# Lighter VectorE steps in the opening, and state-space matrices loaded as whole rows and turned by TensorE, in a two-layer encoder kernel

## The chip, the cores and the metric

The kernel runs on one core of one Trainium2 chip. The metric is the device time of one execution in microseconds (us). The kernel before was timed in three runs: median 1413.44 us, from 1413.34 to 1413.91 us. The profile is of one further execution.

## What is computed

A trunk of two layers over 256 tokens of width 1024, all in float32:

```python
for layer in range(2):
    proj = rms_norm(x) @ w_in[layer]            # q, k, v, u and two gates
    q, k = rotary(q), rotary(k)
    a = diff_attention(q, k, v, lam)            # 4 heads, two softmaxes, lam scales the second
    s = s5_bidirectional(u, ...)                # 32 groups of 16 channels, 64 complex states each
    x = x + (gates[0] * (a @ w_branch[0]) + gates[1] * (glu(s) @ w_branch[1])) @ w_out
    x = x + (swiglu(rms_norm(x)) if layer == 0 else top2_of_8_experts(rms_norm(x)))
out = rms_norm(x)
```

The state-space mixer is where the change lies. For each direction d, group g and state p it has a decay `a_bar = exp(lam * dt)`, an input matrix `b_bar = ((a_bar - 1) / lam) * b_mat` (state by channel) and an output matrix `c_mat` (channel by state):

```python
bu = einsum('gph,bsgh->bsgp', b_bar, u)
states = scan(a_bar, bu)                        # one direction runs backwards
y = u * d_skip + real(einsum('ghp,bsgp->bsgh', c_mat, states))
```

`lam` of the attention is `exp(sum(lp[0]*lp[1])) - exp(sum(lp[2]*lp[3])) + lam_init`, a number for each layer.

## The kernel before, in words

Weights come as tiles of 128x2048 through three raw buffers. ScalarE (ACT) rounds each to a part `hi` (`split`, L1215), VectorE (DVE) makes the rest `lo` (L1632), and TensorE (PE) multiplies with three matmuls for each product (`three`, L659; `proj`, L678). The DMA of a tile waits until the tile three places before it has its `lo` (L543). Tiles 0 and 1 of the opening are the columns of u, 2 and 3 those of v, 4 and 5 of q, 6 and 7 of k, 8 and later of the gates. Each engine has its own program, written out in order; semaphores join them.

The scan is done in chunks of four tokens, so powers 0 to 4 of `a_bar` times the input matrices are needed, and powers 0 to 3 times the output matrices. In layer 0 the powers of the input matrices are made on DVE (`input_power`, L1739), those of the output matrices on POOL (`c_chain`, L2234). In layer 1 POOL makes both.

The opening, layer 0, engine by engine, as far as the change and the prediction touch it:

- POOL issues eight DMAs with the input matrices in runs of 16 numbers (`load_matrices(0)`, L2211), four with the output matrices, each matrix twice (`load_states`, L2217), and four with the skip weights (`load_dskip`, L2224). Then it waits for `par`, makes phasors (`phasors`, L452), the powers of the output matrices, more phasors and the first rotation table (`phase_products`, L2242), and signals `wtab_half` (L2255).
- ACT copies the input matrices into the PSUM banks PY (L1373), and the turned output matrices out of the turn banks TR, two copies of 64 partitions for each bank (`state_numbers`, L1301).
- PE multiplies tiles 0 and 1, turns the seven rows of parameters ("par", L843), multiplies tile 2, turns the output matrices (`states_numbers_t`, L793, 16 transposes of 128x128 in four banks), multiplies tile 3, turns u, multiplies tiles 4 to 7, turns the rotated q, and runs `inner` (L754), which waits for `b_part`, `kdiag_ready` and `c_ready`. Then it turns the rotated k and, in eight banks, the powers (L870, the B turns).
- DVE makes the parameters, splits tiles 2 and 3, makes the attention's lambda sums (L1998, L1999), copies the turned parameters to SBUF (L2002), and goes into `mixer(0)` (L1827): the four factors (`next_factor`), powers 0 and 1, tile 4, power 2, tiles 5 and 6, `rotary` of q, tile 7, powers 3 and 4, the diagonal of the skip weights (`inner_diagonal`, L1758: two operations of 16 partitions), `rotary` of k, tiles 8 and 9.
- ACT in the B turns stops after the fourth one for `scan_tables(0)` (L1321), which waits for `wtab_half`, and copies the rest afterwards.

`rotary` (L1682) reads a projection from its PSUM bank PJ, writes one product of 512 columns and one crossed product of 2x256 to SBUF, gives PJ free for the next projection (`pj_free`, L1698), and adds the two. The output matrices of layer 1 are turned near the end of layer 0's mixer, between the tiles 22 and 23 (L935).

Of the kernel before, what the change touches and what calls it, by code (L numbers as in the profile page):

```python
# [18 lines left out]
P = 128  # L19
# [3 lines left out]
HEADS, HD = 4, 64  # L23
# [19 lines left out]
C_ID, C_TRI, C_ONE, C_IOTA, C_SEL, C_COS, C_SIN = 0, 128, 256, 384, 513, 641, 769  # L43
C_ROW, C_SLOT, C_END = 897, 899, 900
# [79 lines left out]
def build(nc, x, norm_mix, w_in, attn_lambda, attn_subln, ssm_lam_re, ssm_lam_im, ssm_log_dt, ssm_b_re, ssm_b_im,  # L124
# [6 lines left out]
    with ctx:  # L131
# [66 lines left out]
        braw, bbar = powers(area(0, 1024)), powers(area(TMP + 2048, 1024))  # L198
        bt = [powers(area(1024 + 1024 * i, 1024)) for i in range(2)]
        pt = [powers(area(c0, 1024)) for c0 in (14592, TMP)]  # L200
        craw = [area(c0, 1024).rearrange("p (i a s) -> p i a s", i=8, a=2) for c0 in (8192, TMP + 1024)]
# [206 lines left out]
        dve_mark, power_mark = small[:, 20:21], small[:, 21:22]  # L408
        dve_rows, sel_early, inv_ready = sem("dve_rows"), sem("sel_early"), sem("inv_ready")
        B_LOADS, C_LOADS = 16 * 8, 16 * 4  # L410
# [244 lines left out]
        def _(pe):  # L655
# [137 lines left out]
            def states_numbers_t(l):  # L793

                pe.wait_ge(c_in, C_LOADS * (l + 1))
                for g in range(4):
                    transposes((l, "ct", g), [craw[g // 2][:, 4 * (g % 2) + i, :, :].rearrange("p a s -> p (a s)") for i in range(4)])
# [34 lines left out]
            def mixer(l):  # L832
# [375 lines left out]
        def _(act):  # L1208
# [132 lines left out]
            def mixer(l):  # L1341
# [284 lines left out]
        def _(dve):  # L1626
# [55 lines left out]
            def rotary(l, name, dst):  # L1682
                i = place_of(l, name)

                cos_t, sin_t = (cst[:, c:c + 128].rearrange("p (t c) -> p t c", t=2) for c in (C_COS, C_SIN))
                for th in range(TH):
# [5 lines left out]
                    own.step(stt(a_flat[:, 0:512].rearrange("p (h c) -> p h c", c=HD), src.rearrange("p (h c) -> p h c", c=HD),  # L1692
# [721 lines left out]
```

## Time and profile before

| | us |
|---|---|
| median of 3 runs | 1413.44 |
| lowest and highest | 1413.34, 1413.91 |
| the profiled execution | 1413.13 |
| its span, first to last instruction | 1411.3 |
| PE busy | 1371.2 (97%) |
| DVE busy | 1107.8 (78%) |
| ACT busy | 895.1 (63%) |
| POOL busy | 358.3 (25%) |
| mean granted TensorE clock | 0.996 of full |

Busy time of PE counts matmuls in a pipeline from issue to modelled end, so 97% is not the peak. The parts of an engine's time that matter are those which the chain of work that ended last goes through. PEld is PE's weight load. In a line of the trace `out<-in` names the tensors (most of the SBUF areas of the mixer lie in `raw`, `gates` and `areg`), and `[... <-X]` is idle time before the instruction and what ended it.

### The profile page before, as it was taken

Reading aid. Unit: us, or ns where it says so; the run is one execution under the profiler, and the core shown is the slowest. Engines: PE = TensorE matmul, PEld = TensorE weight load, DVE = VectorE, ACT = ScalarE, POOL = GpSimd, SP = SyncE. Lnnn points to the kernel's source line nnn. Section 1 sums busy time; section 2 is a strip of 40 time slices with the busy share of each in tenths; the row PEclk is TensorE's granted clock in tenths of the full one; section 3 lists DMA queues with packets and bytes.
Section 4 is the critical chain, followed back from the end, with each engine's and each line's share of the span. In section 5 each row is a group of like instructions: output and inputs, shape, how many; then the busy total and the mean of one; then the engine's idle time right before and its main releaser. Section 6 shows DMA issues by size and latency. Waiting matters only on the chain.

```text
span 1411.3 us, 23368 instructions
## 1 busy us (share of the span) xinstructions
PE 1371.2 (97%) x8481; PEld 1122.8 (80%) x8481; DVE 1107.8 (78%) x1021; ACT 895.1 (63%) x903; POOL 358.3 (25%) x459
## 2 busy tenths in 40 slices
PE   6889999999999999999999999999999999999996
PEld 4778778788888787788888888888888888888885
DVE  6987677655556587678888888889888888898886
ACT  5445555444445455556777777777777777777775
POOL 4988718996000187000000000000000000000100
PEclk9999999999999999999999999999999999999998
DMA  9433365655545242697999999999999999999991
GB/s 243 159 95 130 113 187 164 207 181 193 193 168 189 57 172 91 235 330 283 365 373 371 389 377 378 386 359 386 384 365 389 382 373 386 360 383 352 384 355 30
DMA packets 194804, 385.16 MB, mean 273 GB/s; under 512 B 17969, under 2 KB 57265, under 8 KB 194610
## 3 DMA queue, kind: packets, MB, share of 16 engines
q1 hardware_dynamic: 188256, 367.51, 72.9%
q0 software_dynamic: 4336, 14.17, 4.0%
q10 hardware_dynamic: 2146, 2.59, 0.6%
q8 instruction: 43, 0.70, 0.2%
q14 instruction: 23, 0.19, 0.0%
HBM read 375.83 MB, written 7.34 MB: 272 GB/s over the span
## 4 chain that ended last, share of the span: by engine, by line
PE 88%; DVE 5%; ACT 3%; issue 2%; DMA 1%; ACTq 0%; POOL 0%; SPq 0%; DVEq 0%; POOLq 0%
PE bank L657 84%; DVE lo L1632 2%; ACT hi L1215 2%; PE bank L1109 1%; PE bank L675 1%; DMA raw<-in_w_in_dram 1%; PE bank L776 1%; DVE raw L1749 0%; PE bank L1092 0%; DVE bank L1751 0%; PE bank L814 0%; DMA areg<-in_norm_mix_dram 0%; PE bank L983 0%; ACT at_hi L1539 0%; DVE areg L1695 0%
## 5 line engine op out<-in xcount | busy, mean ns | idle before, releaser
L1632 DVE TENSOR_TENSOR lo<-raw,hi 128x2048 fp32r<-128x2048 f32 x347 | 803.1, 2326 | 161.3 <-ACT hi L1215 159.1
L1215 ACT ACTIVATE hi<-raw 128x2048 fp32r<-128x2048 f32 x347 | 663.8, 1916 | 183.9 <-PE bank L657 178.1
L657 PE MATMUL bank<-hi,at_hi 128*128 128x512 f32 x1288 | 513.5, 399 | 13.3 <-DVE lo L1632 8.0
L657 PE MATMUL bank<-hi,at_lo 128*128 128x512 f32 x1288 | 503.4, 391 | 0.0
L657 PE MATMUL bank<-lo,at_hi 128*128 128x512 f32 x1288 | 502.6, 390 | 0.0
L657 PEld LDWEIGHTS bank<-hi,at_hi 128*128 128x128 f32 x1288 | 242.5, 188 | 67.9 <-DVE lo L1632 13.3
L657 PEld LDWEIGHTS bank<-hi,at_lo 128*128 128x128 f32 x1288 | 242.1, 188 | 52.1
L657 PEld LDWEIGHTS bank<-lo,at_hi 128*128 128x128 f32 x1288 | 242.7, 188 | 47.3
L657 PE MATMUL bank<-hi,ht_hi 128*128 128x512 f32 x432 | 168.8, 391 | 0.9 <-DVE ht_lo L2116 0.9
L657 PE MATMUL bank<-hi,ht_lo 128*128 128x512 f32 x432 | 168.1, 389 | 0.0
L657 PE MATMUL bank<-lo,ht_hi 128*128 128x512 f32 x432 | 168.1, 389 | 0.0
L2343 POOL TENSOR_TENSOR small<-cst 128x1 f32<-128x1 f32 x14 | 5.9, 422 | 590.7 <-DVE slot_row L2153 298.6
L657 PEld LDWEIGHTS bank<-hi,ht_hi 128*128 128x128 f32 x432 | 81.1, 188 | 19.2 <-DVE lo L1632 1.5
L657 PEld LDWEIGHTS bank<-hi,ht_lo 128*128 128x128 f32 x432 | 81.1, 188 | 17.0
L657 PEld LDWEIGHTS bank<-lo,ht_hi 128*128 128x128 f32 x432 | 81.1, 188 | 16.6
L1548 ACT ACTIVATE ht_hi<-bank 128x512 fp32r<-128x512 f32 (+1 forms) x48 | 26.9, 560 | 55.6 <-PE bank L1109 55.6
L2273 POOL TENSOR_TENSOR raw<-raw 128x256 f32<-128x256 f32 x64 | 46.8, 762 | 21.6 <-ACT raw L1332 7.6
L1544 ACT ACTIVATE vreg<-bank 128x512 f32<-128x512 f32 (+1 forms) x48 | 27.1, 565 | 25.1 <-PE bank L657 25.1
L657 PEld LDWEIGHTS bank<-raw 64*64 64x64 f32 x1152 | 36.1, 134 | 7.6 <-issue 4.4
L657 PE MATMUL bank<-raw 64*64 64x64 f32 x1152 | 40.5, 221 | 0.0
L2266 POOL MEMSET raw<- 128x4 f32 x4 | 0.3, 104 | 151.9 <-DVE raw L1726 151.9
L1227 ACT ACTIVATE at_hi<-bank 128x512 fp32r<-128x512 f32 x32 | 17.7, 596 | 33.3 <-PE bank L675 33.3
(304 smaller groups left out, 1150.8 us busy)
## 6 DMA issues: line engine op xcount, KB each, us to landing
raw<-in_moe_w_dram SPq DMA_DIRECT2D x528, 512.0 KB, 6.8
raw<-in_ffn_w_dram SPq DMA_DIRECT2D x66, 512.0 KB, 4.2
raw<-in_w_in_dram SPq DMA_DIRECT2D x64, 512.0 KB, 4.5
raw<-in_w_branch_dram SPq DMA_DIRECT2D x16, 512.0 KB, 4.4
raw<-in_w_out_dram SPq DMA_DIRECT2D x16, 512.0 KB, 4.7
raw<-in_w_glu_dram SPq DMA_DIRECT2D x4, 512.0 KB, 4.1
moe_sum<-xres POOLq DMA_DIRECT2D x3, 512.0 KB, 5.4
xres<-in_x_dram SPq DMA_DIRECT2D x2, 512.0 KB, 6.5
```

Source lines behind the costliest of these rows:

```text
L657: return pe.matmul(o, a, b, start=start, stop=stop)
L675: last = pe.transpose(bank[:, i * rows:(i + 1) * rows], src, ident[0:rows, 0:rows])
L776: m = pe.matmul(bank[r0:r0 + GC, c0:c0 + 64], bbar[rows, r, q, d, :], cblk[rows, r, q, 4 * d:4 * d + 4, :].rearrange("p i h -> p (i h)"), ...
L1109: m = pe.transpose(TR[0][:, f * P:(f + 1) * P], v_flat[:, f * P:(f + 1) * P], ident)
L1215: act.activation(hi[:, slot, :], src, ACT.Copy).then_inc(hi_ready, 1)
L1227: act.activation(at_hi[:, k0:k0 + kn, c0:c0 + P], bank[:, 0:kn * P].rearrange("p (k c) -> p k c", k=kn), ACT.Copy, scale=scale).then_inc(a ...
L1544: act.activation(v_flat[:, 0:h_width(c)], PJ[0][:, 0:h_width(c)], ACT.Silu).then_inc(g_ready, 1)
L1548: act.activation(ht_rows_hi[:, 0:h_width(c) // P, :], TR[0][:, 0:h_width(c)].rearrange("p (f s) -> p f s", s=P), ACT.Copy).then_inc(ht_hi_ ...
L1632: tt(lo[:, slot, :], src, hi[:, slot, :].bitcast(f32), SUB).then_inc(lo_ready, 1)
L2266: pool.memset(edge[:, :, :, 0:1], 0.0)
L2273: last = tt(dst, src[:, :, :, d, :], w[:, r:r + 1, :, d, :].broadcast_to([P, 2, 2, 64]), MUL)
L2343: tt(small[:, 82 + i:83 + i], ident[:, 0:1], ident[:, 0:1], MUL).then_inc(pool_passed, 1)
```

## The change

- **Input matrices, layer 0.** Two DMAs, one for each of the real and imaginary parts, bring whole rows of 4 KB to 64 partitions each (`brow`). PE turns them with 64 matmuls against columns of the identity straight into the banks PY (`raw_matrices`, between tile 1 and "par"). ACT's two copies into PY go. Layer 1 keeps its eight DMAs.
- **Output matrices, both layers.** Each is loaded once, by two DMAs in place of four. PE turns each bank with eight matmuls of 64 columns, which put the even and odd groups on the two halves of the partitions, in place of four transposes. ACT then copies a bank at once.
- **Parameters.** The copy of the turned parameters goes from DVE to ACT.
- **Lambda.** The sums go from DVE to POOL (seven small operations), before POOL waits for "par"; DVE waits for them ahead of power 1 in layer 0. The last steps of lambda on DVE move behind the first row maximum.
- **Rotary.** The crossed product is made first, the other one in place in the PSUM bank, and the sum is made from both. The bank is given free after the sum, by a memset of its own.
- **Skip diagonal.** One operation of 128 partitions in place of two of 16; the skip weights are cleared once by POOL.

```diff
-        craw = [area(c0, 1024).rearrange("p (i a s) -> p i a s", i=8, a=2) for c0 in (8192, TMP + 1024)]
+        craw = [area(c0, 512).rearrange("p (i s) -> p i s", i=8) for c0 in (8192, TMP + 1024)]
+        brow = area(0, 1024).rearrange("p (s h) -> p s h", h=GC)
...
                 pe.wait_ge(c_in, C_LOADS * (l + 1))
                 for g in range(4):
-                    transposes((l, "ct", g), [craw[g // 2][:, 4 * (g % 2) + i, :, :].rearrange("p a s -> p (a s)") for i in range(4)])
+                    bank = open_turn((l, "ct", g))
+                    for i in range(4):
+                        for odd in range(2):
+                            m = mm(bank[64 * odd:64 * odd + 64, 64 * i:64 * i + 64], craw[g // 2][:, 4 * (g % 2) + i, :],
+                                   ident.rearrange("p (j g h) -> p j g h", g=2, h=GC)[:, :, odd, :], True, True)
+                    m.then_inc(tr_full, 1)
+
+            def raw_matrices():
+
+                pe.wait_ge(b_in, B_LOADS[0])
+                for r in range(2):
+                    rows = slice(64 * r, 64 * r + 64)
+                    for h in range(GC):
+                        for g in range(2):
+                            o = PY[r][64 * g:64 * g + 64, :].rearrange("p (q d h) -> p d q h", q=PAIRS, d=2)[:, :, :, h]
+                            m = mm(o, brow[rows, :, h], ident[rows, 64 * r + g:64 * r + 64:2], True, True)
+                    m.then_inc(braw_full, 1)
...
                 if l == 0:
+                    raw_matrices()
                     pe.wait_ge(dve_par, 1)
...
-                    for odd in range(2):
-                        rows = slice(64 * odd, 64 * (odd + 1))
-                        m = act.activation(cblk[rows, r, :, 7 * d, :],
-                                           bank[rows, :].rearrange("p (j g h) -> p j g h", g=2, h=GC)[:, :, odd, :],
-                                           ACT.Copy, scale=1.0 if r == 0 else -1.0)
+                    m = act.activation(cblk[:, r, :, 7 * d, :], bank[:, 0:256].rearrange("p (q h) -> p q h", h=GC),
+                                       ACT.Copy, scale=1.0 if r == 0 else -1.0)
...
-                    act.wait_ge(b_in, B_LOADS)
-                    for r in range(2):
-                        act.activation(PY[r][:, :], braw[:, r].rearrange("p q d h -> p (q d h)"), ACT.Copy).then_inc(braw_full, 1)
+                    bank = wait_turn(act, "par")
+                    act.activation(par[:, :, :].rearrange("p i (l q d) -> p (i l) q d", l=2, q=PAIRS),
+                                   bank[:, 0:448].rearrange("p (x d q) -> p x q d", d=2, q=PAIRS),
+                                   ACT.Copy).then_inc(tr_free[TURN["par"] % 2], 1)
                     state_numbers(0)
...
-                    own.step(stt(a_flat[:, 0:512].rearrange("p (h c) -> p h c", c=HD), src.rearrange("p (h c) -> p h c", c=HD),
-                                 col(RI + th), cos_t[:, th, :].unsqueeze(1).broadcast_to([P, 8, HD]), MUL, MUL))
+                    crossed = a_flat[:, 512 * th:512 * th + 512]
                     for a in range(2):
-                        m = stt(a_flat[:, 512:1024].rearrange("p (h a c) -> p h a c", a=2, c=32)[:, :, a, :],
+                        m = stt(crossed.rearrange("p (h a c) -> p h a c", a=2, c=32)[:, :, a, :],
                                 src.rearrange("p (h a c) -> p h a c", a=2, c=32)[:, :, 1 - a, :], col(RI + th),
                                 sin_t[:, th, 32 * a:32 * (a + 1)].unsqueeze(1).broadcast_to([P, 8, 32]), MUL, MUL)
-                    m.then_inc(pj_free[th], 1)
-                    dve.wait_ge(pj_free[th], pj_read(l, i))
-                    tt(dst[:, th, :], a_flat[:, 0:512], a_flat[:, 512:1024], ADD).then_inc(rot_ready, 1)
+                    own.step(m)
+                    halves = src.rearrange("p (h c) -> p h c", c=32)
+                    own.step(stt(halves, halves, col(RI + th), cos_t[:, th, :].unsqueeze(1).broadcast_to([P, 16, 32]), MUL, MUL))
+                    tt(dst[:, th, :], src, crossed, ADD).then_inc(rot_ready, 1)
                     dve.wait_ge(rot_ready, 4 * l + (0 if name == "q" else 2) + th + 1)
+                    dve.memset(bank_mark, 0.0).then_inc(pj_free[th], 1)
...
-                for g in range(2):
-                    rows = slice(64 * g, 64 * g + GC)
-                    last = tt(kdiag[rows], cst[rows, C_ID + 64 * g:C_ID + 64 * g + GC].unsqueeze(1).broadcast_to([GC, PAIRS, GC]),
-                              dskip[rows, l, :].unsqueeze(2).broadcast_to([GC, PAIRS, GC]), MUL)
-                last.then_inc(kdiag_ready, 1)
+                tt(kdiag, cst[:, C_UNIT:C_UNIT + GC].unsqueeze(1).broadcast_to([P, PAIRS, GC]),
+                   dskip[:, l, :].unsqueeze(2).broadcast_to([P, PAIRS, GC]), MUL).then_inc(kdiag_ready, 1)
...
                     wait_read(dve, (0, "ct", 3))
+                    dve.wait_ge(lam_ready, 1)
                     input_power(b_power(1), 1)
...
-            dve.wait_ge(lam_in, 32)
-            own.step(tt(lamp.rearrange("p (l a) c -> p l a c", l=2), lamv[:, :, :, 0, :], lamv[:, :, :, 1, :], MUL))
-            dve.tensor_reduce(col(LSUM, 4), lamp, AX.X, ADD).then_inc(lam_ready, 1)
             dve.wait_ge(loads, 16)
-            bank = wait_turn(dve, "par")
-            dve.tensor_copy(par[:, :, :].rearrange("p i (l q d) -> p (i l) q d", l=2, q=PAIRS),
-                            bank[:, 0:448].rearrange("p (x d q) -> p x q d", d=2, q=PAIRS)).then_inc(tr_free[TURN["par"] % 2], 1)
...
-                    for a in range(2):
-
-                        pool.dma_start(craw[r][:, :, a, :], src[l, :, :, :, :].rearrange("d g h s -> (d g h) s")
-                                       .rearrange("(i p) s -> p i s", p=P)).then_inc(c_in, 16)
+                    pool.dma_start(craw[r], src[l, :, :, :, :].rearrange("d g h s -> (d g h) s")
+                                   .rearrange("(i p) s -> p i s", p=P)).then_inc(c_in, 16)
...
-            load_matrices(0)
+            for r, src in enumerate((ssm_b_re, ssm_b_im)):
+                pool.dma_start(brow[64 * r:64 * r + 64, :, :],
+                               src[0, :, :, :, :].rearrange("d g s h -> (d g) s h")).then_inc(b_in, 16)
...
+            own.step(pool.memset(dskip[:, :, :], 0.0))
             load_dskip(0)
             load_dskip(1)
+            pool.wait_ge(lam_in, 32)
+            own.step(tt(lamp.rearrange("p (l a) c -> p l a c", l=2), lamv[:, :, :, 0, :], lamv[:, :, :, 1, :], MUL))
+            for w in (32, 16, 8, 4, 2):
+                own.step(tt(lamp[:, :, 0:w], lamp[:, :, 0:w], lamp[:, :, w:2 * w], ADD))
+            tt(col(LSUM, 4), lamp[:, :, 0], lamp[:, :, 1], ADD).then_inc(lam_ready, 1)
             wait_read(pool, "par")
```

## Rows read from the trace of the kernel before

**Rows 1.** The page, the chain that ended last, shares of the span by engine.

```profile
PE 88%; DVE 5%; ACT 3%; issue 2%; DMA 1%; ACTq 0%; POOL 0%; SPq 0%; DVEq 0%; POOLq 0%
```

**Rows 2.** The chain in order of time: start us, us, what.

```profile
17.57 13.00 DMA raw<-in_w_in_dram
...
221.69 0.45 PE bank L675 x4
...
224.44 5.49 PE bank L657 x24
```

**Rows 3.** Timeline of DVE, layer 0: start us, busy us, operation, [idle before].

```profile
32.53 2.29 DVE L1632 TENSOR_TENSOR lo<-raw,hi 128x2048 fp32r<-128x2048 f32 x1 [0.70 <-ACT hi L1215]
34.74 0.42 DVE L1998 TENSOR_TENSOR gates<-gates 128x256 f32<-128x256 f32 x1
...
35.53 0.61 DVE L2002 COPY par<-bank 128x448 f32<-128x448 f32 x1
...
43.77 1.29 DVE L1749 TENSOR_TENSOR raw<-bank,raw 128x512 f32<-128x512 f32 x2
...
60.48 0.75 DVE L1692 SCALAR_TENSOR_TENSOR areg<-bank,small,cst 128x512 f32<-128x512 f32 x1
61.26 0.88 DVE L1695 SCALAR_TENSOR_TENSOR areg<-bank,small,cst 128x256 f32<-128x256 f32 x2
62.17 1.05 DVE L1700 TENSOR_TENSOR qk<-areg 128x512 f32<-128x512 f32 x1
...
77.11 1.62 DVE L1765 TENSOR_TENSOR raw<-cst,small 16x256 f32<-16x256 f32 x2
```

**Rows 4.** Timeline of PE, layer 0.

```profile
31.01 0.65 PE L675 MATMUL bank<-cst,gates 64*128 64x64 f32 x7
33.22 0.47 PE L657 MATMUL bank<-hi,at_hi 128*128 128x512 f32 x1 [1.55 <-ACT ureg L1266]
...
40.23 1.45 PE L675 MATMUL bank<-cst,raw 128*128 128x128 f32 x8 [0.42 <-ACT raw L1308]
...
47.08 1.99 PE L657 MATMUL bank<-cst,ureg 64*32 64x64 f32 x128
...
78.99 0.33 PE L767 MATMUL bank<-raw,cst 16*16 16x64 f32 x8 [3.14 <-DVE raw L1765]
79.25 3.52 PE L776 MATMUL bank<-raw 64*16 64x64 f32 x128
...
88.75 2.06 PE L657 MATMUL bank<-cst,gates 64*64 64x64 f32 x64
```

**Rows 5.** Stretches: us, busy of PE, PEld, DVE, ACT, POOL; PEclk; DMA share; GB/s.

```profile
26.00:28.00 2.00, 2.00 (x11) 1.65 (x10) 1.83 (x8) 0.89 (x2) 2.00 (x5) 1.00 1.08 147
...
80.00:81.00 1.00, 1.00 (x48) 1.00 (x44) 0.97 (x3) 0.00 (x0) 1.00 (x2) 0.50 0.00 0
```

**Rows 6.** Groups of weight loads by form, to 300 us: busy us, mean ns.

```profile
L657 PEld LDWEIGHTS bank<-cst,gates 64*64 64x64 f32 x192 | 5.8, 135 | 0.0
```

**Rows 7.** Timeline of ACT, layer 0.

```profile
39.41 3.14 ACT L1308 ACTIVATE raw<-bank 64x256 f32<-64x256 f32 x8 [4.74 <-PE bank L675]
...
84.16 0.54 ACT L1318 ACTIVATE areg<-bank 128x448 f32<-128x448 f32 x1 [7.63 <-DVE qk L1700]
...
91.65 0.50 ACT L1332 ACTIVATE raw<-raw 128x128 f32<-128x128 f32 x2
...
109.64 0.38 ACT L1283 ACTIVATE qk<-bank 128x256 f32<-128x256 f32 x1
```

**Rows 8.** Timeline of POOL, layer 0.

```profile
84.35 4.85 POOL L423 TENSOR_TENSOR php_last<-raw 128x128 f32<-128x128 f32 x2
...
89.70 0.45 POOL L2255 TENSOR_TENSOR raw<-php_last 128x128 f32<-128x128 f32 x1
```

**Rows 9.** Layer 1, timelines of DVE and of PE.

```profile
461.30 0.69 DVE L1700 TENSOR_TENSOR qk<-areg 128x512 f32<-128x512 f32 x1
...
461.42 0.47 PE L657 MATMUL bank<-hi,at_hi 128*128 128x512 f32 x1 [0.62 <-DVE areg L1695]
```

More of the change, by code:

```diff
@@ L41 @@
 T_MIX = (0, T_MIX1)
-C_ID, C_TRI, C_ONE, C_IOTA, C_SEL, C_COS, C_SIN = 0, 128, 256, 384, 513, 641, 769
-C_ROW, C_SLOT, C_END = 897, 899, 900
+C_ID, C_TRI, C_ONE, C_IOTA, C_SEL, C_COS, C_SIN = 0, 128, 256, 384, 513, 641, 705
+C_ROW, C_SLOT, C_UNIT, C_END = 833, 835, 836, 852
 GROUPS = (0, 2, 1, 3)
@@ L407, in build @@
         xn_hi, xn_lo = (a[:, (T_MOE + 2) % SPLITS, :].rearrange("p (t d) -> p t d", t=TH) for a in (hi, lo))
-        dve_mark, power_mark = small[:, 20:21], small[:, 21:22]
+        dve_mark, power_mark, bank_mark = small[:, 20:21], small[:, 21:22], small[:, 18:19]
         dve_rows, sel_early, inv_ready = sem("dve_rows"), sem("sel_early"), sem("inv_ready")
-        B_LOADS, C_LOADS = 16 * 8, 16 * 4
+        B_LOADS, C_LOADS = (16 * 2, 16 * 10), 16 * 2
         den_ready, radius_ready, c_in = sem("den_ready"), sem("radius_ready"), sem("c_in")
@@ L1683, in rotary @@
                 i = place_of(l, name)
-                cos_t, sin_t = (cst[:, c:c + 128].rearrange("p (t c) -> p t c", t=2) for c in (C_COS, C_SIN))
+                cos_t = cst[:, C_COS:C_COS + HD].rearrange("p (t c) -> p t c", t=2)
+                sin_t = cst[:, C_SIN:C_SIN + P].rearrange("p (t c) -> p t c", t=2)
                 for th in range(TH):
@@ L1861, in mixer @@
                 scanned(l, 0)
-                if l == 0:
-                    dve.wait_ge(lam_exp, 1)
-                    le = col(LEXP, 4).rearrange("p (l a) -> p l a", l=2)
-                    own.step(tt(col(NLAM, 2), le[:, :, 1], le[:, :, 0], SUB))
-                    for i in range(2):
-                        lam_init = 0.8 - 0.6 * math.exp(-0.3 * i)
-                        own.step(ts(col(NLAM + i), col(NLAM + i), -lam_init, None, ADD))
-                        own.step(ts(subln[:, i, :], subln[:, i, :], 1.0 - lam_init, None, MUL))
                 for s in range(8):
                     row_max(l, s)
+                    if l == 0 and s == 0:
+                        dve.wait_ge(lam_exp, 1)
+                        le = col(LEXP, 4).rearrange("p (l a) -> p l a", l=2)
+                        own.step(tt(col(NLAM, 2), le[:, :, 1], le[:, :, 0], SUB))
+                        for i in range(2):
+                            lam_init = 0.8 - 0.6 * math.exp(-0.3 * i)
+                            own.step(ts(col(NLAM + i), col(NLAM + i), -lam_init, None, ADD))
+                            own.step(ts(subln[:, i, :], subln[:, i, :], 1.0 - lam_init, None, MUL))
                     if s in LOOP_PROJ[l] and s < 7:
@@ L2302, in _ @@
                     pool.wait_ge(at_lo_ready, at_count(0, "m", 3))
-                    pool.wait_ge(b_in, B_LOADS * 2)
+                    pool.wait_ge(b_in, B_LOADS[1])
                 phasors(pool, own, l, (area(14592, 512), area(15104, 512)), php_last, 1, 3)
@@ L2387, in shape_constants @@
     c[:, C_SLOT] = np.arange(P)
+    for g in range(2):
+        c[64 * g:64 * g + GC, C_UNIT:C_UNIT + GC] = np.eye(GC)
     c[:, C_ROW:C_ROW + TH] = SEQ - P * np.arange(TH) - np.arange(P)[:, None]
@@ L2392, in shape_constants @@
     ang = (pos[:, :, None] * freq).astype(np.float32).astype(np.float64)
-    c[:, C_COS:C_COS + P] = np.concatenate([np.cos(ang), np.cos(ang)], -1).reshape(P, P)
+    c[:, C_COS:C_COS + HD] = np.cos(ang).reshape(P, HD)
     c[:, C_SIN:C_SIN + P] = np.concatenate([-np.sin(ang), np.sin(ang)], -1).reshape(P, P)
```

## The prediction, made before the changed kernel was run

> **What bounds the kernel now.** The page comes first. PE has 97% of the span busy and 88% of the chain that ended last [rows 1], so a step counts only where that chain leaves PE, or where PE itself gets more or less to do. The chain in order of time shows three such places. In the opening it runs over DVE from 32.5 us until `inner` starts on PE at 78.99 us, with 3.14 us of idle PE before it [rows 3, 4]. Near the end of layer 0's mixer it goes through the turn of layer 1's output matrices, from 221.69 to 224.44 us [rows 2]. In layer 1 PE waits 0.62 us for DVE's rotary to give a bank free [rows 9]. Elsewhere PE follows itself, so a shift made at these three places should reach the end whole.
>
> **The change, part by part.** Shifts count from the profiled execution (1413.13 us, span 1411.3); minus is earlier.
>
> *Parameters, layer 0.* DVE now ends tile 3 at 34.8, makes lambda sums (34.74 to 35.5) and copies `par` until 36.16 [rows 3]. Afterwards `par` hangs on PE: 64 small matmuls are put in front of the seven turns at 31.01. The trace has no matmul of 64 rows, 64 columns and 32 moving columns. The nearest is 64x64 with 64 moving: 64 in 2.06 us, 32 ns each [rows 4]. With half the moving columns it could fall to the 16 ns of the 64x32 form (128 in 1.99 us) [rows 4], 1.0 us in all; one after the other, without the pairing of two parts of the array, it is 64 ns, 4.1 us. A weight load shows 135 ns from start to end [rows 6]; 64 of these in a row are 8.6 us. I take 2.0 us, since the form differs least. In a sentence of its own: the Trainium skill (TensorEngine Tiling, "Instruction Overhead") gives every matmul some 60 cycles whatever its free dimension, by which halving the moving columns brings nothing and the 1.0 us end falls away; no row here has 32 moving columns.
>
> So: PE is through "par" at 31.01 + 2.06 + 0.65 = 33.7; ACT's copy (0.54 us for the same 448 columns [rows 7]) ends at 34.3. DVE idles 0.70 us before tile 3 because its DMA took 13.0 us [rows 2, 3], at a time when the DMA engines are full but move only 147 GB/s [rows 5]. Rows of 4 KB in place of runs of 64 bytes, and half the output bytes, should end that idle: DVE done at 34.1. The factors start at 34.3 instead of 36.18: **-1.9** (-1.3 if the tile comes no earlier; +0.2 with 4.1 us of matmuls).
>
> *ACT, DMA and POOL there.* ACT loses its copies into PY, at no gain: the work was ahead of its wait for PE (4.74 us idle [rows 7]). The next matmul group of PE starts at 33.7 instead of 33.22, where it waited 1.55 us for ACT [rows 4]. POOL issues fewer DMAs, then memset, seven lambda steps (estimate 3 us, from its 0.45 for 128 columns [rows 8]) before its wait for "par"; it was idle there, as "par" came at 36.16, and the DVE wait for lambda falls after 41 us. Both cost nothing unless "par" came before 28 us.
>
> *Output matrices.* Before, a bank has four transposes and two ACT copies of 0.39 us (3.14 for eight [rows 7]), and PE waits for them: 2.75 us in layer 1's turn [rows 2], and the like in layer 0 (second half of it 1.45 us after a 0.42 us wait [rows 4]). Now one copy of 128x256 is 0.38 us [rows 7], and eight matmuls at 32 ns are 0.26 us. A bank goes round in about 0.26 + 0.1 + 0.38; two banks interleaved need 2 x 0.74 + 0.15 = 1.65 us. Layer 1's: **-1.1** on PE itself (-0.6 at 64 ns a matmul, +1.6 at 135 ns). Layer 0's: PE is through at 41.0, ACT at 41.4, and DVE reaches power 1 (43.77 before [rows 3]) at 41.9, so it does not wait.
>
> *Rotary of q, layer 0.* Steps were 0.75, 0.88 and 1.05 [rows 3]. The sum now reads one PSUM operand and should take about the 0.69 of layer 1 [rows 9], so a half costs 2.45 with the memset instead of 2.78. The second half starts when PE ends its 12 matmuls (half of 5.49 us [rows 2]) after the first, so only the second half's gain and a trace of the first count: **-0.4** (0 to -0.7). K's rotary lies behind `inner`'s start and beside it.
>
> *Skip diagonal.* 1.62 us for two of 16x256 [rows 3] become one of 128x256. Columns set the time: 0.5 us (0.4 to 1.2): **-1.1** (-0.4 to -1.2). `inner` starts at 78.99 - 3.4 = 75.6. POOL's `c_ready` was no wait at 78.99 and moves forward with "par".
>
> *Clock.* `inner`'s first 128 matmuls took 3.52 us [rows 4] at a granted clock of 0.50 (1.2 GHz) [rows 5], after the 3.14 us of idleness. That idleness shrinks by the diagonal's 1.1 us to 2.0; a 1.55 us idle [rows 4] was followed by no loss. If the clock stays at 2.4 GHz, half of 3.52 goes. K's rotary ends at 84.16 [rows 7] - 3.4 - 0.6 (two sums at 0.69 for 1.05, less the memsets), about 80.1, together with `inner`. The B turns could start 4.3 us earlier.
>
> *POOL is late next.* ACT's rotation tables at 91.65 [rows 7] wait for POOL's 89.70 + 0.45 = 90.15 [rows 8], now 1.5 us to spare. A POOL operation of 128 columns is 0.45 there; the pair of them before took 4.85 us [rows 8], while DVE split two tiles from SBUF, so POOL gets through about a fifth of its work under splits. The splits now fall at 80.1 to 84.9. POOL, only 1.9 us ahead, would reach that pair at 84.35 - 1.9 = 82.45; so at 80.1 it has 2.35 + 0.9 + 0.9 = 4.15 us of work left, does 0.95 of it under the splits and ends at 84.9 + 3.2 = 88.1. ACT wants it at 91.65 - 4.3 = 87.35. So the opening keeps **-3.5**, not -4.3.
>
> *Rotary, layer 1.* The bank is given free after the sum instead of before: 0.69 [rows 9] plus the memset, **+0.75** on PE once, at 461.4 (0.6 to 0.9). The k one has PE behind in other work.
>
> **Sum:** -3.5 - 1.1 + 0.75 = -3.85 us: 1413.13 - 3.85 = 1409.3. The median stood 0.3 above the execution: 1409.6 us.
>
> **The rivals.** A measurement tells 0.2% (2.8 us) from no change: faster is under 1410.6, slower over 1416.3.
>
> (a) *No pairing of the small matmuls*, 64 ns each. Then "par" is ready at 36.4 and layer 0's output turns are read at 43.5, and the clock may still fall: opening -1.6 to -2.2, turn -0.6, rotary +0.75: about 1411.6. For it: all 32 of one part read the same 64 partitions, unlike the B turns. Against: turns of u share rows in pairs and still go at 16 ns. Chance 0.2.
>
> (b) *Weight loads that do not overlap*, the slower side. If consecutive matmuls on the same rows must each wait for their load, with p ns each, power 1 moves by 96p - 6.0 us (64 matmuls, then 32 on the way), the turn of layer 1 by 32p - 2.7, the rest stays -2.9 + 0.75 (p in us there): 128p - 10.85 in all. It is zero at 85 ns, over +2.8 from 107 ns, and +6.4 at the 135 ns of a load [rows 6]: 1419.8. Against: seven turns of "par" on the same 64 rows took 0.65 us together [rows 4], 93 ns each with the tail of the last one. The Trainium skill (TensorE: Matmul & The Clock Gate, "What overlaps and what doesn't") says that a weight load overlaps matmuls in flight only when the row group differs, and `raw_matrices` keeps one row group for 32 matmuls; by that rule this rival holds, and the trace's "par" turns speak against it. Chance 0.08.
>
> (c) *POOL bounds the opening harder*: its phasors fall wholly under the splits, and the opening keeps only the -1.9 that POOL itself gains. Sum -2.3: 1411.1. For it: the 4.85 us pair. Chance 0.14.
>
> (d) *POOL gets through*, and the clock holds: -4.3, or more with 16 ns matmuls; -5 in all: 1408.4. Chance 0.08.
>
> (e) *The whole rows land no earlier*, so that the load part does not do what it says: 0.6 us less, 1410.2, inside the forecast's range. The forecast with it has 0.5.
>
> **How the numbers follow.** Forecast 0.5, 1409.6, own range 1408.8 to 1410.6. Eight in ten needs (d)'s side to 1408.0 and (a) and (c) to 1412.4; left out are (b) and the tails. Faster: 0.45 of the forecast, 0.08 of (d), 0.05 of (c), 0.04 of (a) = 0.62. Slower: 0.07 of (b). Same: 0.31.
>
> **What would show it.** The small matmuls in 2.0 us from 31.0 (4.1: rival a; over 6.8: b). "Par" on ACT ending at 34.3. Tile 3's DMA well under 13 us. `inner` at 75.6 with a clock of 1.00. ACT's idle before the rotation tables ended by POOL, under 1 us. The turn at 221.7 minus the shift in 1.65 us. PE idle 1.4 us before layer 1's k projection. Wrong would be a layer-1 stretch, experts included, whose length between two fixed events changes by more than these terms: then shifts at the front do not reach the end.

## The result, and the profile after the change

The changed kernel takes 1417.61 us (median of 14 runs, 1416.23 to 1421.42) where the kernel before, on the same chips, takes 1413.46 us (14 runs, 1412.34 to 1416.11). The ratio is 1.0031, with a 95% interval of 1.0024 to 1.0038: **slower by some 4 us**, where 3.85 us less had been forecast. Its profiled execution took 1417.19 us with a span of 1415.3 us, against 1411.3 before.

The page's chain of after has the same make-up as before [rows 1]: the place has to be looked for in time, not in shares.

```profile
PE 89%; DVE 5%; ACT 3%; issue 2%; POOL 1%; DMA 0%; ACTq 0%; DVEq 0%; POOLq 0%
```

The chain in order of time (start us, us, what) answers to [rows 2].

```profile
21.98 1.03 PE bank L676 x8
23.01 15.22 PE bank L658 x164
38.24 0.94 PE bank L676 x7
39.17 8.40 PE bank L658 x56
...
47.59 1.18 PE bank L658 x32
...
48.79 0.39 ACT raw L1324
...
49.37 1.29 DVE raw L1767 x2
```

Before, the chain ran through a DMA from 17.57 [rows 2] and then stayed on DVE from 32.53 [rows 3]. Now PE holds it from 16.5 to 48.77 us: PE has become the bound of the opening. The timeline of PE shows with what.

```profile
31.17 7.07 PE L658 MATMUL bank<-cst,raw 64*64 64x32 f32 x128
38.17 1.00 PE L676 MATMUL bank<-cst,gates 64*128 64x64 f32 x7
39.10 0.79 PE L658 MATMUL bank<-hi,at_hi 128*128 128x512 f32 x1
...
46.42 2.32 PE L658 MATMUL bank<-cst,raw 128*64 128x64 f32 x64
...
81.95 0.30 PE L768 MATMUL bank<-raw,cst 16*16 16x64 f32 x8 [1.74 <-DVE raw L1781]
82.18 1.98 PE L777 MATMUL bank<-raw 64*16 64x64 f32 x128
...
86.02 1.51 PE L777 MATMUL bank<-raw 64*16 64x64 f32 x91 [0.97 <-issue]
...
88.90 2.08 PE L658 MATMUL bank<-cst,raw 64*64 64x64 f32 x64 [0.34 <-ACT qk L1488]
```

The 64 matmuls of the input matrices are 128 instructions, and they take 7.07 us, 55 ns an instruction, where 2.0 us had been counted. The turn of the parameters behind them goes from 0.65 [rows 4] to 1.00 us, and the first large matmul from 0.47 to 0.79. The stretches say why (us; busy of PE, PEld, DVE, ACT, POOL; PEclk; DMA share; GB/s).

```profile
34.00:35.00 1.00, 1.00 (x29) 1.00 (x28) 1.00 (x1) 0.15 (x1) 0.00 (x0) 1.00 0.79 264
35.00:36.00 1.00, 1.00 (x22) 1.00 (x22) 0.04 (x1) 0.00 (x0) 0.00 (x0) 0.92 1.05 369
36.00:37.00 1.00, 1.00 (x22) 1.00 (x21) 0.00 (x0) 0.00 (x0) 0.00 (x0) 0.50 0.99 377
...
41.00:42.00 1.00, 1.00 (x4) 0.81 (x3) 0.94 (x4) 0.00 (x0) 0.86 (x3) 0.50 0.00 0
42.00:43.00 1.00, 1.00 (x5) 0.77 (x4) 0.90 (x6) 0.00 (x0) 0.89 (x4) 0.67 0.00 0
```

```profile
39.21 0.54 ACT L1387 ACTIVATE par<-bank 128x448 f32<-128x448 f32 x1 [5.06 <-PE bank L676]
```

```profile
39.85 0.36 DVE L1752 TENSOR_TENSOR raw<-par 128x64 f32<-128x64 f32 x1 [4.81 <-ACT par L1387]
...
49.37 1.29 DVE L1767 TENSOR_TENSOR raw<-bank,raw 128x512 f32<-128x512 f32 x2 [1.62 <-ACT raw L1324]
...
81.27 0.43 DVE L1781 TENSOR_TENSOR raw<-cst,small 128x256 f32<-128x256 f32 x1
```

From the same events in both traces comes the ledger, after minus before:

| event | before | after | shift |
|---|---|---|---|
| DVE begins the factors | 36.18 | 39.85 | +3.67 |
| DVE begins power 1 | 43.77 | 49.37 | +5.60 |
| `inner` of layer 0 begins | 78.99 | 81.95 | +2.96 |
| B turns of layer 0 begin | 86.87 | 88.90 | +2.03 |
| second transposes in the loop (L814, now L831) | 117.82 | 120.56 | +2.74 |
| turn of q near the end of layer 0, past the output matrices | 229.77 | 232.37 | +2.60 |
| k projection of layer 1 | 461.42 | 464.85 | +3.43 |
| span | 1411.3 | 1415.3 | +4.0 |

The opening loses 5.6 us, gets 2.64 back until `inner` (1.19 from the diagonal, 0.47 from the rotary of q, the rest mostly from shorter splits, 2.29 us in place of 2.85 for tile 4) and 0.93 from there to the B turns. The first 128 instructions of `inner` take 1.98 and not 3.52 us [rows 4], which is 1.54, but a wait in its second half is 0.65 us longer than before (0.97 in place of 0.32). From there the B turns take 0.44 us more than before (9.85 in place of 9.41 until the first scores) and the loop 0.27, where PE waits for a GpSimd product. Layer 1's rotary adds 0.86: PE idles 1.48 us there in place of 0.62 [rows 9]. Of the last 0.6 us, 0.33 come between 461 and 492 us, where PE waits in layer 1's `inner`, again for nothing that the profile names, 1.47 us in place of 0.26 and 0.89; the rest comes in small steps up to the end and was not followed.

```profile
464.85 0.47 PE L658 MATMUL bank<-hi,at_hi 128*128 128x512 f32 x1 [1.48 <-DVE small L1719]
```

### The profile page after: what moved, and what is told of

The parts are those of the page before. It is cut to its first block, busy times and chain, and to the rows that moved or that the text cites. A ratio compares the mean times of both kernels' runs of the same rounds, so it can differ in the third digit from the quotient of the medians.

```text
span 1415.3 us, 23801 instructions
## 1 busy us (share of the span) xinstructions
PE 1380.5 (98%) x8705; PEld 1131.0 (80%) x8705; DVE 1101.7 (78%) x1024; ACT 891.0 (63%) x894; POOL 351.2 (25%) x457
## 4 chain that ended last, share of the span: by engine, by line
PE 89%; DVE 5%; ACT 3%; issue 2%; POOL 1%; DMA 0%; ACTq 0%; DVEq 0%; POOLq 0%
PE bank L658 84%; DVE lo L1648 2%; ACT hi L1233 2%; PE bank L1127 1%; PE bank L676 1%; PE bank L777 1%; POOL raw L2281 1%; PE bank L1110 0%; DVE raw L1767 0%; DVE bank L1769 0%; PE bank L1001 0%; ACT at_hi L1555 0%; PE bank L831 0%; DMA areg<-in_norm_mix_dram 0%; ACT at_hi L1245 0%
```

## The experiments

Each time is set against the kernel before on the same chip: 1412.94 us (29 runs) for e1 to e4, 1413.15 us (35 runs) for e5 to e8, 1413.32 us (21 runs) for e9 to e12. The intervals are about 0.0009 wide to either side, 1.3 us, so differences of 1 us between two experiments rest on events in their traces and not on the medians. A trace is of one execution only, and it need not be a typical one: that of e2 took 1410.53 us where the median is 1412.12, that of e12 1410.59 where it is 1412.50, that of e4 1417.73 where it is 1416.17.

**e1: the change without its input matrices.**

```diff
-                    raw_matrices()
+                    act.wait_ge(b_in, B_LOADS[0])
+                    for r in range(2):
+                        act.activation(PY[r][:, :], braw[:, r].rearrange("p q d h -> p (q d h)"), ACT.Copy).then_inc(braw_full, 1)
...
+            load_matrices(0)
```

> The changed kernel with the input matrices of layer 0 as before (eight DMAs, ACT copies them into the banks, after its copy of the parameters); all else as changed. Theory A (the 64 input matmuls cost the time: 7.0 us from 31.17 us on, and everything behind the parameters waits): the parameters are ready near 34.9 us in place of 39.8, the inner part starts at 75 to 77 us instead of 81.95, and the time is 1410 to 1412 us, under the kernel before. Rival B (the loss comes from the rotary and the output matrices, and the input matmuls were hidden): the time stays above 1415 us.

Measured: 1410.79 us (12 runs), ratio 0.9986 [0.9978, 0.9995], 2.15 us under the kernel before. The factors begin at 35.59, power 1 at 42.91, `inner` at 76.38. So this part carries the whole loss, 6.3 us between the changed kernel and this one (+4.15 and -2.15, each against its own reference).

**e11: the kernel before with that part alone.** The edit is the reverse of e1's, made in the kernel before.

> The kernel before with one part of the change: the input matrices as whole rows and the 64 small matmuls, at the same place; the parameters are still copied by VectorE and the output matrices turned as before. Theory A: the block costs the 7.0 us that it takes, and the clock falls behind it. The parameters are ready 3.7 us later and power 1 about 6 us later; nothing else is gained, so the time is about 1419. Theory B: as in the changed kernel some 3 us are won back in the opening by lighter splits on VectorE, whose neighbour GpSimd is then idle: about 1416.5.

Measured: 1419.74 us (4 runs), ratio 1.0047 [1.0032, 1.0063], +6.4 us. The block takes 7.09 us, the clock falls at 36.3, and power 1 starts at 50.73, 7.0 us later than before. Theory A holds. The two sides add up: +6.4 for the part alone and -2.15 for the rest make +4.3, measured +4.15.

**e2: the block alternates between the two halves of the rows.**

```diff
-                for r in range(2):
-                    rows = slice(64 * r, 64 * r + 64)
-                    for h in range(GC):
-                        for g in range(2):
+                for h in range(GC):
+                    for g in range(2):
+                        for r in range(2):
+                            rows = slice(64 * r, 64 * r + 64)
```

> The changed kernel with the 64 input matmuls in another order: the real part (rows 0 to 63) and the imaginary part (rows 64 to 127) alternate. Theory C (a weight load cannot overlap a matmul on the same rows): the block falls from 7.0 us to about 2 to 4.1 us and the time by 3 to 5 us. Rival D (reading the weights in steps of 64 bytes is what is slow): the block stays within 1 us of 7.0. Rival E (a floor of some 45 ns for each instruction): also stays.

**e3: the weights are 64 numbers in a row**, not one in every 16; layer 0's input matrices are then made of other elements.

```diff
-                            m = mm(o, brow[rows, :, h], ident[rows, 64 * r + g:64 * r + 64:2], True, True)
+                            m = mm(o, brow[rows, 4 * h:4 * h + 4, :].rearrange("p s h -> p (s h)"), ident[rows, 64 * r + g:64 * r + 64:2], True, True)
```

> The changed kernel with the 64 input matmuls reading 64 numbers side by side as weights, not in steps of 16 (the input matrices are then not turned rightly in layer 0; the amount of work is the same). Rival D (step of the weights): the block falls from 7.0 us to about 4 us, and its weight loads from some 200 ns to the 135 ns of the others. Theory C (same rows) or E (floor per instruction): the block stays within 1 us of 7.0.

**e9: both at once.**

> The changed kernel with both cures of its block of 64 small matmuls at once: the order alternates between the two halves of the rows (as in e2) and the weights are 64 numbers in a row (as in e3). Layer 0's input matrices are then not the right ones. Theory A: either cure takes away one and the same wait, and what is left is a floor of each instruction: the block takes 3.7 to 3.9 us, as in e2 and e3. Theory B: each cure takes away a cost of its own: the block falls to about 2 us, the 16 ns of the fastest rows. On the clock: theory C, it fell in e3 because one half of the array's rows stood still for 1.9 us at a time, so here it stays at 2.4 GHz, as in e2; theory D, it has to do with the shape of the weights alone, and it falls as in e3.

The block in the timelines of PE of e2, of e3 and of e9:

```profile
31.02 3.85 PE L658 MATMUL bank<-cst,raw 64*64 64x32 f32 x128
```

```profile
31.06 3.72 PE L658 MATMUL bank<-cst,raw 64*64 64x32 f32 x128
```

```profile
30.78 2.07 PE L658 MATMUL bank<-cst,raw 64*64 64x32 f32 x128
```

And its weight loads, by form, after, in e2 and in e3 (busy us, mean ns):

```profile
L658 PEld LDWEIGHTS bank<-cst,raw 64*64 64x64 f32 x128 | 6.9, 204 | 0.4 <-issue 0.4
```

```profile
L658 PEld LDWEIGHTS bank<-cst,raw 64*64 64x64 f32 x128 | 3.7, 204 | 0.4 <-issue 0.4
```

```profile
L658 PEld LDWEIGHTS bank<-cst,raw 64*64 64x64 f32 x128 | 3.6, 135 | 0.4 <-issue 0.4
```

| | same rows in a row | rows alternate |
|---|---|---|
| one weight in 16 | 7.07 us, 55 ns (after) | 3.85 us, 30 ns (e2) |
| weights in a row | 3.72 us, 29 ns (e3) | 2.07 us, 16 ns (e9) |

Each condition costs a factor of about two (1.8 to 1.9), and they multiply. So theory C of e2 and rival D of e3 both hold, though each had been written against the other, rival E falls, and theory B of e9 holds: there are two costs.

A load of spread-out weights takes 204 ns from start to end where a packed one takes 135, as long whether the rows alternate or not (the loads overlap in the trace, so neither figure is what one more load costs). The starts of the single instructions show what is waited for. On the same rows the two instructions of a matmul start some 10 ns apart, and the next matmul 101 ns later with spread-out weights (after) or 52 ns later with packed ones (e3). Where the rows alternate, four instructions start 7 to 10 ns apart, one matmul on each half, and the next four 87 ns (e2) or 38 ns (e9) later. With both cures the block takes the 2.0 us of the forecast.

On the clock (the stretches from 36 us on of e3 and of e2):

```profile
36.00:37.00 1.00, 1.00 (x4) 0.75 (x3) 0.92 (x4) 0.00 (x0) 0.90 (x4) 0.50 1.01 379
```

```profile
36.00:37.00 1.00, 1.00 (x6) 0.83 (x5) 0.82 (x4) 0.04 (x1) 0.81 (x4) 1.00 1.07 389
```

It fell in e3, at 35.6 us for some 3 us, with PE busy, as it did after and in e4 and e11; it did not fall there in the traces of e2 and of e9. e2's block is as long as e3's. In the four traces where it fell, one half of the rows works for 1.9 us or more while the other rests, and in e2 and e9 both work. That fits theory C of e9, but no run shows the mechanism, and two things limit it. e8 and e12, which have no such block, have the clock at 0.50 here as well, from 34.55 and from 33.20 us, when PE had been idle for 2.31 and for 2.65 us; in e1 it had been idle for 2.29 us and the clock stayed. So a fall at this place does not need the block. And of e2 only one execution of ten is traced; two of the others took 1415.3 and 1416.0 us, at a mean granted clock of 0.996 and 0.995 where the traced one had 0.997. In time: e2 1412.12 us (10 runs, ratio 0.9999 [0.9989, 1.0009]), some 5 us under the changed kernel, as theory C had it; e3 1413.0 and e9 1409.86 (one run each). Power 1 starts at 44.01 in e2 and at 45.50 in e3, though both have their parameters by 36.1: the difference is tile 2 at half the clock.

**e4: the turn of the parameters ahead of the block.** The two calls change places.

> The changed kernel with the turn of the parameters ahead of the 64 input matmuls. Theory A: the parameters are ready near 35 us, the input matmuls end at 38.9 and are just in time for VectorE's first product, but the next weight tile, the output matrices and power 1 still wait for them (power 1 at about 48 us instead of 49.4), so only 1 to 1.5 us of the loss comes back: about 1416.2 us. Rival F (only the parameters mattered): power 1 starts at 44.5 us or before and the time is under 1413.5.

Measured: 1416.17 us (10 runs), ratio 1.0023 [1.0013, 1.0032]. The time is theory A's, but power 1 begins at 50.16 and not at 48. DVE now has its parameters at 35.63, as in e1, and gains nothing by it: it idles 6.50 us ahead of power 1. That is 0.8 us later than in the changed kernel's trace, as much as PE was later behind tile 1 ("par" from 32.00, the block there from 31.17). Whether the 0.9 us between the two medians (+3.2 and +4.15) are real, the intervals don't tell.

```profile
39.84 1.29 DVE L1767 TENSOR_TENSOR raw<-bank,par 128x512 f32<-128x512 f32 x2 [0.56 <-PE bank L658]
...
50.16 1.29 DVE L1767 TENSOR_TENSOR raw<-bank,raw 128x512 f32<-128x512 f32 x2 [6.50 <-ACT raw L1324]
```

So the loss does not hang on the place of "par". The second way it goes is PE's own queue: block, then tile 2 at half the clock, then the turn of the output matrices, ACT's copy, power 1.

**e10: the kernel before with the new skip diagonal alone.**

```diff
+                tt(kdiag, cst[:, C_UNIT:C_UNIT + GC].unsqueeze(1).broadcast_to([P, PAIRS, GC]),
+                   dskip[:, l, :].unsqueeze(2).broadcast_to([P, PAIRS, GC]), MUL).then_inc(kdiag_ready, 1)
```

> The kernel before with one part of the change: the skip diagonal in one operation of 128 partitions (for room, the cosines are also stored once, without a step more or less). Theory A, that of the prediction: VectorE gains 1.2 us, the idle time of TensorE ahead of the inner products falls from 3.1 to 2.0 us, their clock stays at 2.4 GHz, and their first 128 instructions take 2.0 in place of 3.5 us: about -2.5 us in all, 1410.6. Theory B: an idle time of 2.0 us is still too long, or the clock goes by more than the idle time; the first 128 take 3.5 us and the gain is 1.2 us, 1411.9.

Measured: 1412.12 us (11 runs), 1.2 us under the kernel before, ratio 0.9996 [0.9987, 1.0005]: theory B's time, though the interval does not tell it from no change. The step takes 0.42 us and `inner` begins 1.26 us earlier, but the clock falls all the same, only later, in the middle of its first half:

```profile
77.73 0.30 PE L767 MATMUL bank<-raw,cst 16*16 16x64 f32 x8 [1.99 <-DVE raw L1764]
77.96 2.68 PE L776 MATMUL bank<-raw 64*16 64x64 f32 x128
80.57 0.41 PE L767 MATMUL bank<-raw,cst 16*16 16x64 f32 x8
80.91 2.69 PE L776 MATMUL bank<-raw 64*16 64x64 f32 x128
```

**e6: e1 with the old turn of the output matrices** (four loads, four transposes and two ACT copies a bank).

```diff
-                    for i in range(4):
-                        for odd in range(2):
-                            m = mm(bank[64 * odd:64 * odd + 64, 64 * i:64 * i + 64], craw[g // 2][:, 4 * (g % 2) + i, :],
-                                   ident.rearrange("p (j g h) -> p j g h", g=2, h=GC)[:, :, odd, :], True, True)
-                    m.then_inc(tr_full, 1)
+                    transposes((l, "ct", g), [craw[g // 2][:, 4 * (g % 2) + i, :, :].rearrange("p a s -> p (a s)") for i in range(4)])
```

> Input matrices as in the kernel before (as in e1), and the output matrices loaded twice, turned by four transposes a bank and copied by two ScalarE steps a bank, as in the kernel before. Theory A: the new turn gains 0.3 us of TensorE's time in layer 1 and nothing in layer 0, where VectorE is not waiting for it: from 1410.8 to about 1411.1. Theory B, that of the prediction: it gains 1.1 us in layer 1: about 1411.9. Theory C: in layer 0 the shorter copies on ScalarE are what let VectorE reach power 1 early; then power 1 starts later than 42.9 us and the time is 1412 or more.

Measured: 1413.13 us (11 runs), ratio 0.9996 [0.9988, 1.0005], as the kernel before. Between the events at 182 and at 228 us it loses 0.31 us to e1 (182.56 less 181.78 is 0.78; 228.13 less 227.04 is 1.09), which is theory A's 0.3 and not the 1.1 of the prediction. But the time is theory C's, and so is its sign: DVE waits 0.94 us for ACT's copies and begins power 1 at 43.58, 0.67 later than in e1. Of these 0.25 us are left at `inner`. The B turns begin 1.52 us later than in e1, so 1.27 are lost within `inner`. Its clock fell, which theory C had not named:

```profile
76.63 0.30 PE L768 MATMUL bank<-raw,cst 16*16 16x64 f32 x8 [1.77 <-DVE raw L1781]
76.86 3.59 PE L777 MATMUL bank<-raw 64*16 64x64 f32 x128
```

against e1:

```profile
76.38 0.30 PE L768 MATMUL bank<-raw,cst 16*16 16x64 f32 x8 [1.67 <-DVE raw L1783]
76.61 1.98 PE L777 MATMUL bank<-raw 64*16 64x64 f32 x128
```

An idle time of 1.77 us and one of 1.67 go with different clocks, and e11 keeps the full clock after a longer one:

```profile
85.46 0.30 PE L768 MATMUL bank<-raw,cst 16*16 16x64 f32 x8 [3.18 <-DVE raw L1775]
85.69 1.98 PE L777 MATMUL bank<-raw 64*16 64x64 f32 x128
```

So the length of the idle time does not decide it. Nor is the clock all of the 1.27 us: e11, which has the old turn of the output matrices too, kept the full clock and still took 6.04 us from the start of `inner` to the turns of k, where e6 took 6.75 and e1 5.49. The clock is thus worth 0.7 us here, and the rest goes with a wait of PE that is taken up in the last section.

**e7, e12 and e5, e8: rotary and lambda, all upon e1.** e7 has the rotary of the kernel before in layer 1, e12 in both layers; e5 has the last lambda steps ahead of the loop again; e8 has both e7's and e5's edits.

```diff
+            def rotary(l, name, dst):
+                (rotary_in_bank if l == 0 else rotary_beside)(l, name, dst)
```

> Input matrices as in the kernel before (as in e1); rotary in the bank in layer 0, but as in the kernel before in layer 1. Theory A: layer 1's late release of the bank costs TensorE 0.86 us, which reach the end: from 1410.8 to about 1409.9, with a wait of 0.6 us ahead of layer 1's k projection in place of 1.4. Theory B: what TensorE gains there it waits for at the inner products of layer 1, which the state-space chain sets: no change, 1410.8.

> The kernel of e1 (changed, with the input matrices as before) with the rotary of the kernel before in both layers; e7 has it in layer 1 alone. Theory A: rotary in the bank gains 0.5 us in layer 0, by its sum of 0.69 in place of 1.05 to 1.11 us, all of it ahead of the inner products: about 1410.5, 0.5 over e7. Theory B: that gain is the layer-0 sum meeting GpSimd's work at another moment, and nothing reaches the end: 1410.0, as e7. If the time is over 1411.5, the clock in the inner products has fallen again.

> Input matrices as in the kernel before (as in e1), and the last lambda steps of VectorE back ahead of the loop over the row maxima. Theory A: these 2.4 us in the loop make the split, the scale and GpSimd's next rotation product late, and TensorE waits for GpSimd. Then the stretch from the first B turn to the transposes of the attention at 115 us falls from 32.0 us (e1) to the 31.0 of the kernel before, and the time from 1410.8 to about 1409.8. Theory B: the stretch is longer because GpSimd's products meet VectorE's splits at other moments, whatever the lambda steps do. Then the stretch stays at 32.0 and the time at 1410.8.

> Input matrices as in the kernel before, layer 1's rotary as in the kernel before, and the last lambda steps ahead of the loop: the change without the parts that were found or suspected to cost time. If the two gains are real and add up: 1410.8 - 0.9 - 1.0 = 1408.9, about 4 us under the kernel before. If only the rotary counts: 1409.9. If neither: 1410.8.

| | median us (runs) | against before | ratio |
|---|---|---|---|
| e5, lambda | 1411.04 (11) | -2.1 | 0.9987 [0.9979, 0.9996] |
| e7, rotary of layer 1 | 1410.04 (12) | -3.1 | 0.9979 [0.9971, 0.9988] |
| e8, both | 1409.95 (11) | -3.2 | 0.9977 [0.9968, 0.9986] |
| e12, rotary of both layers | 1412.50 (11, one of them 4869.63) | -0.8 | 0.9996 [0.9987, 1.0005] |

e7: the wait ahead of layer 1's k projection is 0.62 us again, 0.86 less than in e1, and the median lies 0.96 us further below its kernel before than e1's does: theory A, by the trace, since 0.96 is within the noise of two medians. The 0.86 us are still there at 1380 us. e5: the wait for GpSimd is gone from the loop, and the stretch from the first B turn to the transposes near 115 us is 31.4 us, between the two theories. But e7, with the lambda steps still in the loop, has no such wait either, and e8 is no faster than e7 beyond the noise (its trace has the clock loss in the opening that was told above, and e7's has not): what is lost by that wait is 0.27 us where it shows (10.20 between two transposes in place of 9.93), and whether it shows does not follow the lambda steps. Theory A of e5 falls. e12: layer 0's rotary of q is 0.5 us longer than in the bank (5.67 against 5.16 us for both halves), as theory A says, and the time is over 1411.5. The clock in `inner` fell in its trace (3.29 us for the first 128 instructions, after 1.95 us of idleness), as the expectation had it; but that trace is of the fastest execution, 1410.59 us, and its `inner` took 5.80 us up to the turns of k, as long as e8's at the full clock. So what makes the median 2 us slower than e7's is not shown.

**e8 beats both kernels**: 3.2 us under the one before and 7.4 under the changed one, each against its own reference. It is the change without the input matrices and with layer 1's old rotary; the lambda steps make no difference that the medians can tell (e7 against e8).

## Why the prediction was wrong

The sum was -3.5 - 1.1 + 0.75. The outcome is +4.15 by the medians: 1417.6 us, above the upper end of the range, 1412.4, and with the other sign. In the terms of the sum, from the ledger: the opening is +2.0 at the B turns in place of -3.5, the turn of layer 1 is -0.3 in place of -1.1, the rotary +0.86 in place of +0.75, and 0.7 in layer 0's B turns and loop and 0.3 in layer 1's `inner` were in no term.

- **The 64 small matmuls: the step that failed.** The prediction took "64 in 2.06 us, 32 ns each" as the nearest row and wrote 2.0 us. Two things are wrong in it. The x64 of that row counts instructions, and a float32 matmul that is no transpose is two of them: `inner` issues 64 matmuls for a bank and its row says x128. So that row is 64 ns a matmul, and 32 moving columns happen to halve it again (16 ns an instruction in e9); the two slips cancel. (So the prediction's sentence that halving the moving columns brings nothing does not hold here: 32 ns with 64 columns, 16 with 32.) What does not cancel is that the row has neither of the block's two conditions, the same rows one after the other and weights spread by 16. Each doubles the time (the table of e2, e3 and e9), and 2.07 becomes 7.07. The turns of u, named against rival (a) as sharing rows in pairs, do not have the conditions either: their inner loop changes the half with every matmul.
- **Rival (b) was the outcome.** It asked p ns for each matmul on the same rows, and gave 128p - 10.85. With the measured p of 110 ns (two instructions of 55) that is +3.2 us; measured +4.15. That it comes so near is in part luck, since the output turns took only 72 ns a matmul and the rival has no term for the clock: 64 matmuls at 110 ns and 32 at 72, less 6.0, move power 1 by +3.3, the clock adds 2.2, and +5.60 was measured. It had 0.08, because the seven turns of "par" on the same rows went at 93 ns. They are transposes, one instruction each, and with packed weights: a row without the block's second condition, and perhaps too few to show the first. The rule of the Trainium skill cited there (TensorE: Matmul & The Clock Gate, "What overlaps and what doesn't") says that a weight load overlaps matmuls in flight only when the row group differs. The traces agree: 29 ns on the same rows and 16 when they alternate. It does not speak of spread-out weights, which is the other half of the cost.
- **What was late next.** "PE is through at 41.0 ... so it does not wait" took the output turn as covered. It ended at 48.7. Two paths lead from the block to DVE, and with "par" moved to the front the other one alone kept the loss (e4).
- **A clock loss that was not looked for.** The prediction watched the clock behind idle PE. It fell while PE was busy all the time, 4.7 us into the block. The 24 large matmuls of tile 2 took 7.32 us (39.10 to 46.42) where 24 take 5.49 at full clock [rows 2], and the turn of "par" took 0.35 us more: 2.2 us in PE's queue, all of it on the way to power 1.
- **Output matrices, layer 1.** -1.1 was forecast, -0.3 measured. A bank has eight matmuls, thus 16 instructions of 36 ns, and PE itself is the bound: 64 of them in 2.32 us. The "-0.6 at 64 ns a matmul" of the same sentence was the better one.
- **Skip diagonal.** Right: 0.43 us in place of 1.62, -1.19, and by itself (e10) `inner` begins 1.26 us earlier; the median is 1.2 us lower, which is within the noise.
- **Rotary.** Right in both layers: -0.5 for q (forecast -0.4), +0.86 in layer 1 (forecast +0.75, and it reaches the end in the trace of e7).
- **Clock in `inner`.** Forecast to hold, and it held, but not for the reason given: e6, e9, e10 and e12 lost it after 1.77 to 1.99 us of idleness, e11 kept it after 3.18. The lower clock makes the first 128 instructions 1.3 to 1.6 us longer (0.7 in e10, where it fell in the middle), but it costs less than that in time, since the wait in the second half is shorter where they were slow. From the start of `inner` to the turns of k it took 5.4 to 5.8 us at the full clock (6.0 in e11), and 6.44 (before), 6.75 (e6) and 5.80 to 5.84 (e9, e10, e12) where the clock fell. No experiment says what makes it fall or stay, and that it held was in this sense luck.
- **GpSimd late at the tables.** Not so: its table was ready at 93.22 and ACT began at 93.38 without a wait in the trace, with 0.16 us to spare. So rival (c) falls. The condition of rival (d) came true, GpSimd through in time and the clock held; its price, which stood on the opening, did not.
- **DMA of tile 3.** Its idle time of 0.70 us did go, but its split began at 32.76 in place of 32.53, since DVE was busy with the parameters until 30.3. The rows did land earlier, as the forecast had it and rival (e) had not: ACT could begin to round the tile at 28.17 in place of 30.59. It was of no use.

## What to carry to other kernels

Before small float32 matmuls are priced by a row of the trace, count the instructions of the row against the matmuls of the source, and compare three more things than the shape: whether neighbours use the same rows, whether the weights lie packed, and what is queued behind them on PE. Alternate the halves of the rows, and have the weights packed; here each was worth a factor of two. (To put the spread-out operand on the moving side is one way to packed weights, but no run here did that, and e3 and e9 packed them at the price of other numbers.) And when a block is put into an engine's queue, follow every path out of it, since taking one consumer off it may save nothing.

## What the runs showed of the hardware that was not expected

- Packed and spread-out weights: a load of 64x64 numbers takes 135 ns packed and 204 ns with one number in 16 (e3, after). In a row of matmuls on the same rows this is the difference between 29 and 55 ns an instruction.
- Two float32 matmuls of 64x64 weights on different halves of the rows start within some 10 ns of each other, and the next two 87 ns (e2) or 38 ns (e9) later; on one and the same half each waits 101 ns (after) or 52 ns (e3) behind the one before.
- TensorE's granted clock fell from 2.4 to 1.2 GHz while PE was busy without a gap, within or behind a block of small matmuls that used one half of the rows at a time (after, e3, e4, e11), and it did not where the halves alternated (one trace each of e2 and e9).
- The small matmuls themselves went equally fast at either clock (22 instructions touch a slice of a microsecond both at 33 and at 36 us).
- The clock behind an idle time of PE is not told by its length: full after 3.18 us (e11), half after 1.77 us (e6). What decides it stays open.
- In the second half of `inner` PE waits 0.3 to 1.5 us for nothing that the profile names, always at one and the same instruction of a kernel: after the 85th of the second bank before, in e6 and in e11, after the 37th in the changed kernel and in e1 to e5, e7 and e8. In each of these eleven traces PE goes on 1.3 to 1.6 us after a packet of 16 KB of the queue that the profile calls `q8 instruction` has landed (at 84.59 in the changed kernel, PE at 86.02). In e9, e10 and e12 there is no wait, and there the packet had landed 1.6 to 1.9 us before PE came to that instruction. So PE seems to wait for the next part of its program; that is read from the times alone, and no experiment changed it. It would also account for a slower clock in the first half costing less time than it adds there.
